# Local attention with the values as weights, its output born turned, and output products from the first mixer scores on

## The reference, cut to what matters

```python
s = jnp.einsum('bnqhgd,bnkhd->bnhgqk', qb, kw) * (1.0 / math.sqrt(HEAD_DIM))   # blocks of 128, window of 3 blocks
m = jnp.maximum(jnp.max(s, axis=-1, keepdims=True), sink_l)
p = jnp.exp(s - m)
denom = jnp.sum(p, axis=-1, keepdims=True) + jnp.exp(sink_l - m)
o = jnp.einsum('bnhgqk,bnkhd->bnqhgd', (p / denom), vw)                        # 8 heads of 64, 2 key heads
y_att = rms_norm(o, att_g)                                                     # over 512 columns per token
y = jnp.concatenate([y_att, y_ml], axis=-1) @ w_out
x = layer_norm(ALPHA * x + y, ln1_g, ln1_b)
```

## Time and profile before

| | |
|---|---|
| median of 3 runs | 2194.73 us (2194.62 to 2200.78) |
| the profiled execution, its own time | 2202.17 us |
| its span | 2200.5 us |
| mean granted TensorE clock | 0.981 |
| TensorE matmul, weight load, VectorE, ScalarE, GpSimd busy | 95%, 76%, 60%, 45%, 10% of the span |
| attention of layer 0, of layer 1 | about 80 to 262 us, 1145 to 1327 us |
| mLSTM groups of layer 0, of layer 1 | about 263 to 361 us, 1328 to 1424 us |

### The profile page before, as it was taken

The page is one execution under the profiler, slowest core; times in us unless marked ns, Lnnn a source line. Parts: engine busy times, 40 slices in busy tenths (PEclk is TensorE's granted clock), DMA queues, the critical chain, the costliest instruction groups (busy, mean ns, idle before and its releaser), DMA issues.

```text
span 2200.5 us, 30134 instructions
## 1 busy us (share of the span) xinstructions
PE 2094.4 (95%) x10816; PEld 1666.4 (76%) x10816; DVE 1320.6 (60%) x2013; ACT 979.7 (45%) x1570; POOL 225.8 (10%) x268
## 2 busy tenths in 40 slices
PE   7999999999998899999799999999999989999998
PEld 6888777878877677777588886788888767777774
DVE  3785577731455665565868647782335376665567
ACT  3555665232422355555246556523333135555553
POOL 0000032000001321000100002300000032100004
PEclk9999999999998899999899998999999899999999
DMA  4164202321103699999511012123210069999996
GB/s 155 58 225 140 100 20 86 107 96 39 58 29 151 236 354 378 385 382 346 190 58 44 34 39 96 44 111 115 77 58 20 34 231 383 371 378 375 375 386 231
DMA packets 78526, 384.78 MB, mean 175 GB/s; under 512 B 10472, under 2 KB 11864, under 8 KB 43608
## 3 DMA queue, kind: packets, MB, share of 16 engines
q1 hardware_dynamic: 55264, 327.31, 39.2%
q0 software_dynamic: 10096, 30.38, 3.9%
q10 hardware_dynamic: 13064, 25.75, 3.2%
HBM read 352.27 MB, written 46.07 MB: 181 GB/s over the span
## 4 chain that ended last, share of the span: by engine, by line
PE 79%; DVE 11%; ACT 5%; issue 2%; DMA 2%; POOL 0%; DVEq 0%; ACTq 0%; SPq 0%; POOLq 0%
PE bank L2245 32%; PE bank L2767 10%; PE bank L2741 8%; PE bank L2731 7%; PE bank L2468 5%; PE bank L2440 2%; PE bank L2499 2%; PE bank L2578 2%; PE bank L2266 1%; DVE weight_slots_parts L1471 1%; PE bank L2707 1%; PE bank L2622 1%; DVE weight_slots_parts L1951 1%; PE bank L2638 1%; PE bank L2661 1%
## 5 line engine op out<-in xcount | busy, mean ns | idle before, releaser
L1951 DVE TENSOR_TENSOR weight_slots_parts<-weight_slots,mixer_region_parts 128x2048 fp32r<-128x2048 f32 x140 | 322.6, 2325 | 85.6 <-ACT mixer_region_parts L1295 85.5
L2245 PE MATMUL bank<-weight_slots_parts,x_transposed_parts 128*128 128x512 f32 x864 | 279.2, 405 | 1.5 <-DVE weight_slots_parts L1471 1.5
L1295 ACT ACTIVATE mixer_region_parts<-weight_slots 128x2048 fp32r<-128x2048 f32 x140 | 261.0, 1909 | 22.3 <-ACT x_transposed L1370 18.1
L2245 PE MATMUL bank<-x_transposed_parts,weight_slots_parts 128*128 128x512 f32 (+1 forms) x1024 | 259.2, 340 | 3.8 <-DVE mixer_region_parts L1440 2.7
L1471 DVE TENSOR_TENSOR weight_slots_parts<-weight_slots,weight_slots_parts 128x2048 fp32r<-128x2048 f32 x58 | 133.0, 2292 | 196.8 <-ACT weight_slots_parts L980 196.0
L2767 PE MATMUL bank<-weight_slots,x_transposed 128*128 128x512 f32 x560 | 248.1, 596 | 0.0
L2741 PE MATMUL bank<-mixer_region_parts,x_transposed_parts 128*128 128x256 f32 x1120 | 207.6, 283 | 0.6 <-DVE weight_slots_parts L1951 0.5
L2731 PE MATMUL bank<-mixer_region_parts,x_transposed_parts 128*128 128x512 f32 x560 | 192.1, 414 | 5.4 <-ACTq L1335 2.3
L2245 PEld LDWEIGHTS bank<-x_transposed_parts,weight_slots_parts 128*128 128x128 f32 x1024 | 177.1, 189 | 25.1 <-issue 3.6
L2767 PEld LDWEIGHTS bank<-weight_slots,x_transposed 128*128 128x128 f32 x560 | 104.2, 191 | 118.9 <-issue 103.4
L2245 PEld LDWEIGHTS bank<-weight_slots_parts,x_transposed_parts 128*128 128x128 f32 x864 | 162.5, 194 | 34.2 <-DVE weight_slots_parts L1471 2.3
(11 more groups left out here) (322 smaller groups left out, 3521.5 us busy)
## 6 DMA issues: line engine op xcount, KB each, us to landing
weight_slots<-in_w_gate SPq DMA_DIRECT2D x70, 1024.0 KB, 7.3
weight_slots<-in_w_up SPq DMA_DIRECT2D x70, 1024.0 KB, 7.1
weight_slots<-in_w_down SPq DMA_DIRECT2D x70, 1024.0 KB, 7.6
weight_slots<-in_w_in SPq DMA_DIRECT2D x20, 1024.0 KB, 4.9
slots_y<-x_transposed ACTq DMA_DIRECT2D x66, 256.0 KB, 7.2
weight_slots<-in_wkv_mem SPq DMA_DIRECT2D x16, 1024.0 KB, 4.8
slots_y<-in_consts SPq DMA_DIRECT2D x6, 2304.0 KB, 16.4
weight_slots<-in_w_out SPq DMA_DIRECT2D x8, 1024.0 KB, 5.0
```

Of the source, the lines that this page charges most:

```text
L1295: nc.scalar.activation(hi, raw, ACT.Copy).then_inc(moe.high_ready, 1)
L1951: v.tensor_tensor(lo, raw, hi.bitcast(F32), ALU.subtract).then_inc(moe.low_ready, 1)
L2245: ins = pe.matmul(ps, lhs[i](k), rhs[j](k), start=k == 0 and a == 0, stop=k == KD - 1 and a == 2)
```

## The change

Six things change together.

1. In the product with the values the operands change places: the 64 columns of values of one key head are stationary, and the probabilities of two heads, 256 columns, move. The output has the head's 64 dimensions on the partitions: key head 0 on partitions 0 to 63, key head 1 on 64 to 127. An item has 2 x (key blocks) products, 4 or 6, instead of 8 or 12.
2. The division by the softmax sums needs them along the free axis. VectorE's reciprocals (four per token) are spread by GpSimd to 128 x 256 (`share_rows`), turned by two transposes on TensorE (`("sr", i-1)`), copied out by ScalarE (`shares`) and multiplied into the product by VectorE.
3. The attention half is now turned from birth: its 24 transposes are gone; its high parts are ScalarE copies and its low parts VectorE subtractions, both from SBUF. Two chunks (`ATT_AHEAD`) are done in turn 11 of the attention loop, the other four in the first group.
4. The norm's factor per token is applied behind the product, when VectorE adds it to `x` (`attention_half`); the gain goes into `w_out` (`wo0`, `wo1`: four ScalarE copies with a scale and four VectorE instructions in place of one each). The sums of squares: ScalarE squares, VectorE adds four lanes (`sum_squares`), TensorE adds the partitions (`sum_tokens`, one column each, `("rs", part)`), ScalarE takes the root.
5. `early_steps` gives one step at every point from the first on, 45 in all, and three behind the loop.
6. The high and low parts of `wo0` come one stream tile earlier.

```diff
-YT_BEHIND = ((), (0, 1, 2, 3), (4,), (5,))
+ATT_AHEAD = 2
...
 def early_steps(point):
-    return max(0, ML_POINTS.index(point) + 1 - CHUNKS[0])
+    return min(ML_POINTS.index(point) + 1, EARLY_STEPS - 3)
...
         if i:
+            add(("sr", i - 1), (4, 5))
             add(("pv", i - 1), (4, 5))
...
+SPLIT_BEHIND[("o", 5, 0)] = SPLIT_BEHIND.pop(("o", 3, 1))
@@ GpSimd @@
+                    for i in range(12):
+                        pool.wait_ge(shares_ready, 12 * l + i + 1)
+                        nc.gpsimd.tensor_copy(share_rows.rearrange("p (t d) -> p t d", t=GRP),
+                                              st[:, 110:114].unsqueeze(2).broadcast_to([P, GRP, HD])).then_inc(ones_made, 1)
@@ ScalarE @@
+                        elif name in ("wo0", "wo1"):
...
+                            for j in range(GRP - 1):
+                                nc.scalar.activation(hi[:, j, :], raw[:, j, :], ACT.Copy, scale=lane_gain[:, j:j + 1])
...
                     def square_of(c):
                         tile_drained(act, ("pv", 2 * c + 1))
-                        act.wait_ge(cv_used, 16 * l + 16)
-                        step(nc.scalar.activation(esc[:, :], y[:, c, 0:ATT], ACT.Square, accum_out=st[:, 20 + c:21 + c]))
+                        if c < NC - 1:
+                            tile_filled(act, ("sc", 2 * c + 1, len(score_tiles(2 * c + 1)) - 1))
+                            out = qT[:, :, c * P:(c + 1) * P]
+                        else:
+                            act.wait_ge(cv_used, 16 * l + 16)
+                            tile_filled(act, ("rs", 0))
+                            out = esc[:, :].rearrange("p (j t) -> p j t", j=GRP)
+                        nc.scalar.activation(out, y_turned[:, c, 0:GRP, :], ACT.Square).then_inc(turned, 1)
...
+                    def high_y(c):
+                        tile_filled(act, STREAM[-1] if c >= ATT_AHEAD else ("o", c, 1))
+                        nc.scalar.activation(x_hi[:, 0:GRP, c * P:(c + 1) * P], y_turned[:, c, 0:GRP, :], ACT.Copy).then_inc(turned, 1)
...
+                        if i:
+                            if i > 1:
+                                tile_drained(act, ("pv", i - 2))
+                            drain_copy(("sr", i - 1), shares, 2 * P)
                         if 7 <= i < 12:
                             square_of(i - 7)
                         if i == 11:
-                            rstd(st[:, 20:25], st[:, 20:25], 5, 1.0 / ATT, eps_rms).then_inc(att_rs, 1)
+                            for c in range(ATT_AHEAD):
+                                high_y(c)
...
+                        if g == 1:
+                            attention_rstd(0, 0, NC - 1)
+                            attention_rstd(1, NC - 1, 1)
@@ VectorE @@
+                    def sum_squares(c):
+                        dve.wait_ge(turned, len(TURNED) * now[0] + TURNED[("squares", c)] + 1)
...
+                        v.tensor_reduce(sums_at(c), sq.rearrange("p j t -> p t j"), AX.X, ALU.add).then_inc(att_parts, 1)
...
-                            step(v.reciprocal(st[:, ro:ro + 4], st[:, ro:ro + 4]))
+                            v.reciprocal(st[:, 110:114], st[:, 110:114]).then_inc(shares_ready, 1)
...
-                        if i == 12:
-                            dve.wait_ge(att_rs, 2 * l + 1)
-                            for c in range(NC - 1):
-                                attention_scaled(c)
...
+                            tile_drained(dve, ("sr", i - 1))
+                            v.tensor_tensor(y[:, c, 2 * P * jp:2 * P * (jp + 1)], bank_of(key)[:, 0:2 * P], shares, ALU.mult).then_inc(drain_sem(key), 1)
...
+                        if i >= 8:
+                            sum_squares(i - 8)
...
+                        if i == 11:
+                            for c in range(ATT_AHEAD):
+                                low_y_attention(c)
...
+                    def attention_half(h, c):
...
+                        v.scalar_tensor_tensor(out=xh, in0=bank_of(key)[:, :], scalar=st[:, 20 + c:21 + c], in1=xh,
+                                               op0=ALU.mult, op1=ALU.add).then_inc(drain_sem(key), 1)
...
                                 if g == 0:
-                                    for c in ((), (0, 1), (2, 3), (4, 5))[sc]:
-                                        low_y(c, 0)
+                                    for c in ((), (2,), (3, 4), (5,))[sc]:
+                                        low_y_attention(c)
@@ TensorE @@
+                            pe.wait_ge(ones_made, 13 * l + 1 + i)
+                            ps = take(("sr", i - 1))
+                            for j in range(2):
+                                ins = pe.transpose(ps[:, j * P:(j + 1) * P], share_rows[:, j * P:(j + 1) * P], ident)
...
-                            for t in range(GRP):
-                                n, _ = head_at(jp, t)
-                                for k in range(nb):
-                                    ins = pe.matmul(ps[:, t * HD:(t + 1) * HD], ptb[:, (t * nb + k) * P:(t * nb + k + 1) * P],
-                                                    kv[:, k0 + k, NKV * HD + n * HD:NKV * HD + (n + 1) * HD],
+                            for k in range(nb):
+                                for n in range(NKV):
+                                    out = ps[n * HD:(n + 1) * HD, 0:2 * P].rearrange("p (j q) -> p j q", j=2)
+                                    mine = ptb[:, 0:GRP * nb * P].rearrange("p (j n k q) -> p n k j q", j=2, n=NKV, k=nb)[:, n, k, :, :]
+                                    ins = pe.matmul(out, kv[:, k0 + k, NKV * HD + n * HD:NKV * HD + (n + 1) * HD], mine,
                                                     start=(k == 0), stop=(k == nb - 1))
...
+                        for c in range(c0, c0 + n):
+                            pe.wait_ge(att_parts, 12 * l + ATT_PARTS[("sum", c)] + 1)
+                            ins = pe.matmul(ps[:, c - c0:c - c0 + 1], sums_at(c), one, start=True, stop=True)
...
+                    sum_tokens(0, 0, NC - 1)
...
                                 early_sum(early_steps((g, "st", sc)))
-                                for c in YT_BEHIND[sc] if g == 0 else ():
-                                    pe.wait_ge(y_att, 6 * l + c + 1)
-                                    turn4(("yt", c, 0), lambda k: y[:, c, k * P:(k + 1) * P])
+                            if g == 0:
+                                sum_tokens(1, NC - 1, 1)
```

133 lines of the change are left out of this document (90 added, 43 removed).

## The result

The changed kernel takes 2217.79 us (median of four runs, 2213.46 to 2219.67) against 2196.69 us before: ratio 1.0081, interval 1.0061 to 1.0101. Over six more runs it was 2217.75 us, ratio 1.0086 (1.0068 to 1.0103). It is slower by 18 to 21 us, by the ratios and by the medians; 2186.3 was forecast, with 2209 as the upper end. The traced execution has a span of 2211.8 us against 2200.5, so its trace shows 11 us of the difference. It was the fastest of its four runs (2213.46), and the traced execution of before (2202.17) lies above the median of before.

A forecast was written before the change was run, and what follows sets the result against it. TensorE's work was taken to bound the attention loop, a VectorE and ScalarE chain the tail. Loop -4.7 and tail with end +0.5 us per layer, twice, made -8.4 us: 2186.3 us, range 2176 to 2209.

The forecast's parts named there:

- The value products: Attention loop, TensorE: column halves share the array, 1.07 and 1.60 us an item, saving 8.2 us per layer.
- The first rival: Value products: column halves don't share the array, +0.3 us an item, +15 us in all, 2209.5; chance 0.23.
- The transposes: Attention loop, TensorE: two transposes of the spread reciprocals per item, 0.25 us each item, 2.75 us for eleven.
- It starts at VectorE's reciprocal, ... so it costs nothing in turns 1 to 11 at either bound: Attention loop: GpSimd's copy, taken as 0.6 us, is hidden because TensorE wants it a stream tile later, 2.85 us.
- The slack given to ScalarE's copy: Attention loop: the 0.39 us copy delays sigmoids and weight parts by at most about 0.4 us, covered by ScalarE's idle time.
- the first items' gain: Loop, 103 to 116 us: VectorE is as full as TensorE, so 2 x 0.38 us of gain is not had.
- The tail: 257 to 292 us: added VectorE and ScalarE steps, TensorE idle 5.7 us, next group +1.7 us.
- The larger parts of `wo1` stand beside TensorE work of a group: Groups: 0.6 us more on each of two engines, taken as hidden beside TensorE's work.
- The end of the groups: End of the groups: earlier output steps bring the last residual and `wo2`'s low part forward, -1.2 us per layer.
- The sum: Both layers: loop -4.7 and tail with end +0.5 us each, -8.4 us in all, 2186.3 us from the median.
- signs of being wrong altogether: Loop not shorter by about 5 us per layer, or groups from the second on running at another pace.
- The sign of the first rival: Value product with 64 stationary columns: 1.8 to 2.0 us to the next row for 8 records, against 1.1 forecast.

The follow-up runs named there:

- one_half: Changed kernel with value products key head by key head, both heads on the lower 64 output partitions, upper half left out; 8 records 1.87 us, single run 2211.1 us.
- warm: Changed kernel plus 13 extra products that nothing reads, in turn 12 where TensorE waits 6.15 us for GpSimd; 2233.4 us, ratio 1.0159.
- wo1_plain: Changed kernel with `wo1` split as before, one ScalarE and one VectorE instruction, its gains left out; 2204.7 us, ratio 1.0036.

## Why the prediction was wrong, step by step

**The value products: right.** The 8 records take 1.01 us and the 12 take 1.45 (1.07 and 1.60 forecast), and the reason given, shared halves, is shown by one_half. The rule of the Trainium skill that only row groups let a weight load overlap ("TensorE: Matmul & The Clock Gate", Part 3) would add a load to each of the eight records, on top of 8 x 0.22 = 1.77 us; the measurement disagrees. Even on one half the 1.87 us leave almost no room for loads. The first rival, whose time of 2209.5 lies nearest to the result, has the wrong cause: only a kernel with both heads on one half shows its price.

**The transposes**: 0.32 us an item for 0.25, 0.8 us per layer more.

**"It starts at VectorE's reciprocal, ... so it costs nothing in turns 1 to 11 at either bound": this step failed.** I bounded GpSimd's copy (0.40 us, under 0.6) and not the moment at which VectorE comes to the reciprocal. In turn 1 that is 6 us after the exponentials. TensorE waits 1.95 us for 0.57, and the clock falls: 2.6 us until the scores of item 2 (105.92 for 103.54, from starts at 80.66 and 80.86). With the reciprocal moved the loop gains 3.8 of the 4.7 forecast; as it stands it gains 1.0. The slack given to ScalarE's copy wasn't all there either: at 229.72 TensorE waits 1.40 us for the low part of a weight, where it waited 0.73 before, because ScalarE starts the high part 1.10 us after the exponentials and not 0.78, and TensorE comes sooner. I had even cut the first items' gain because VectorE is full in that stretch, and didn't see that a full VectorE also delays what it starts.

**The tail: right in kind, too small.** The line-up of single instructions gave 5.7 us idle and the first scores at 273.9; they were 6.15 and 274.71. What failed is the way from there: counted from the loop's end the first value tile comes 5.2 us later, outside 0 to +2.9, and the next group 4.9 and 4.3 us later in the two layers, outside 0 to +3.2, of which I took +1.7. The half clock was priced at 3 us and taken as partly hidden. The mean clock from 269 to 278 was 0.50, VectorE's first decay products waited for the scores until 276.86, and the first value tile then stood behind ScalarE (0.36 us, L1110). How much of the miss is the clock's isn't settled (warm).

**"The larger parts of `wo1` stand beside TensorE work of a group": this step failed.** 0.6 us was set down as hidden; the four instructions meet GpSimd's products, take 2.5 us longer and stall TensorE twice: 2 us per layer, by wo1_plain.

**The end of the groups**: -1.2 was forecast for the output steps given out earlier, none found. The last value tile waits 1.15 us for VectorE, since no output steps are left to stand ahead of it, and GpSimd's product sets the transposes in any case (1.85 us idle for 0.46).

**The sum.** Per layer -1.0 + 4.6 + 1.9 = +5.5 in the first trace, for -4.7 + 0.5; 11 us in two layers. Runs at half clock in turn 3 add up to 3. The medians differ by 18 to 21, and what is left, 4 to 10 us, I can't place in one stretch. Part of it can be the choice of executions: the second traces of both kernels (2222.27 and 2200.65 us) are 21.6 us apart, 14.8 in the stretches and 6.8 in the rest, which lies between 1635 and 1645 us over all kernels with the right values, the two traces of before at 1638. Whether the change makes the rest longer is not shown.

**The signs.** Both signs of being wrong altogether came: the loop is 1.0 us shorter and not 5, and the groups run at another pace. TensorE does wait for GpSimd in turn 1, and the third group starts 47.7 us after the turned probabilities of item 11 (248.20 to 295.88), for 43 to 46. The sign of the first rival, 1.8 to 2.0 us for 8 records, did not come: slower was given 0.21, nearly all for a cause that isn't there.

## What to carry to other kernels

A new hand-over between engines is priced by when its first engine comes to it, not by how long its instructions take: read what is queued ahead of it in the one turn in which that engine is full. A stall of two microseconds on TensorE costs more than itself where the clock falls behind it: 1.6 us more in turn 1. When a long instruction is split into several, look which engine works beside it at that moment.

## What the runs showed of the hardware

- Products with 64 stationary columns on the two output halves: 8 records of 256 columns in 1.02 us, on one half 1.87; 12 in 1.45 when alternating, 1.92 half by half, 2.73 on one half.
- Four VectorE instructions of 128 x 512 took 2.77 us where no two-operand product of GpSimd ran, and 4.76 beside GpSimd's two. One of 128 x 2048 kept its 2.29 us beside them, and GpSimd's first took 2.44 for 1.04.
- Behind the same stall of 1.67 us TensorE's clock fell in some executions of one program and not in others (8 of 22 layers); behind one of 1.95 us in 11 of 14.
